# A two-layer streaming step with four mixers: first loads of POOL behind the first weights, x turned in one go, and 64 stationary columns for the sampled tokens' values

## Chip, cores and metric

One NeuronCore of one Trainium2 chip. The metric is the device time of one execution in microseconds (us), all inputs read from HBM and all outputs written to HBM. Everything is fp32.

## What is computed

The reference runs two layers over 256 prompt tokens and 64 sampled tokens (width 1024), the sampled ones with a cache of 512 latents and with recurrent states. Cut to one layer:

```
h = rms(x, norm_mix);  proj = h @ w_in            # 1024 -> 2984, split into 14 parts
y_a = rglru(causal_conv(lru_x))                   # gated linear recurrence
q = rms(q_lat) @ wq_b;  kv = [past_ckv, rms(kv_lat)] @ wkv_b
y_b = softmax(q k^T) v                            # latent attention, 4 heads
y_c = retention(rope(r_q), rope(r_k), r_v)        # 4 heads, state 64x64
y_d = mlstm(m_q, m_k, m_v, gates)                 # 4 heads, state 64x64
x = x + [head_rms(y_a..y_d) * gates] @ w_out
x = x + (silu(g) * u) @ w_down,  [g, u] = rms(x, norm_ffn) @ w_gu
```

The outputs are x for both token groups and each layer's new latents and states.

## The kernel before

The 320 tokens are kept feature by token: `xT` and `hT` hold 8 tiles of 128 features by 320 tokens. The tokens count as three tiles of 128, the last of which holds the 64 sampled ones and 64 unused places. Weights come in chunks of 256 columns (1 MB, two transfers on SP's queue) into `ring`, which has 5 slots; a slot is loaded again when TensorE has used it. Each engine has its program written out by hand, and semaphores with names order them: `step` makes an engine wait for its own last instruction, `need`, `claim`, `wait_filled` and `wait_chunk` wait for other engines, for a PSUM bank to be read, or for a chunk.

The start of the program is what most of the change touches:

- SP issues the transfers of x (second token tile and sampled tile, in two halves of 512 features: `x_loaded0`, `x_loaded1`), the chunk `ql` (weights of the query latents, the first weights used), seven small row loads, then the chunks `kvr`, `mo`, `mv`, `mq`. ACT issues the first token tile of x and the identity matrix. POOL issues the latents' loads (`load_latents`: `pckv`, `wqb`, `wkvb`), four blocks of the mLSTM state (`cin`), the first part of the constants (680 KB), four small gains, twelve small tables and the rest of the constants (1664 KB). Queue q0 is POOL's, q1 SP's, q10 ACT's.
- PE turns x into PSUM by matmuls with the identity (`turn_x`, L706), DVE copies each turned tile to `xT` (L1552), ACT squares it into `hT` (L1275), and PE sums the squares with a matrix of ones (`first_sum`, L712) into `ms1`. ACT makes `rstd` of that, DVE writes the normalised `hT` tile by tile (L1556), and PE starts on `ql0` and `ql1` (`feature`, L740).
- Then PE turns the rows of small vectors (L835) and the cached latents (`past_latents`, L805), multiplies these with `wkvb` (`latents_out`, L820), turns `cin` (L845), and goes on with `kvr` (L853), `mo`, the gate rows (L863), `mv`, ..., `mq`. Before `mq` it waits for all of the tables.

Later, in each layer, `weigh_values` (from L1017) multiplies the turned softmax weights `pT` with the values `vb` of one head; tile 2, the sampled tokens, takes five matmuls (L1021, L1023), and `b_out` on DVE scales the result into `ybm`. An fp32 matmul shows as two MATMUL records in the trace, and as one row with its repetitions in the lists of order below.

Of the kernel before, what the change touches and what calls it, by code (L numbers as in the profile page):

```python
# [16 lines left out]
ALU = mybir.AluOpType  # L17
# [4 lines left out]
P = 128  # L22
# [180 lines left out]
def build(nc, I, O):  # L203
    with ExitStack() as ctx:
# [15 lines left out]
        def C(name, rows=P):  # L220
            a, n = cat[name]
            return cst[0:rows, a:a + n]
# [119 lines left out]
        rows = gate[0:NROWS, 0, 0:P]  # L342
        cin = dhf[:, 0:DEPTH * 256].rearrange("p (l k a d) -> p l k a d", l=DEPTH, k=2, a=2)
        yst = sb("yst", [P, 6, NT * H])
# [242 lines left out]
        def _(pool):  # L587
# [40 lines left out]
            for l in range(DEPTH):  # L628

                if l == 0:  # L630
                    load_latents(0)
                    pool.wait_ge(sem("cleared_small"), 5)
                    for cdst, csrc in CIN:
                        pool.dma_start(cdst, csrc, allow_slow_non_contiguous=True).then_inc(sem("cin_loaded"), 16)
                    c1 = cat["negmask"][0]
                    pool.dma_start(cst[:, 2 * P:c1], I["consts"][:, 2 * P:c1]).then_inc(sem("consts_loaded"), 16)
                    for cdst, csrc in SMALL[0:4]:
                        pool.dma_start(cdst, csrc, allow_slow_non_contiguous=True).then_inc(sem("gains_loaded"), 16)
# [51 lines left out]
        def _(pe):  # L690
# [7 lines left out]
            for _ in range(WARM):  # L698
                mm(ps[:, 7, 0:P], dmx[:, 0:P], dmx[:, 0:P], start=True, stop=True)
            pe.wait_ge(sem("ident_loaded"), 16)  # L700
            pe.wait_ge(sem("x_cleared"), 1)
            def turn_x(ks):
                pe.wait_ge(sem(f"x_loaded{ks[0] // (KT // 2)}"), 48)
# [5 lines left out]
            def first_sum(ks):  # L709
                for k in ks:  # L710
                    need(pe, "squared", 0, 2 * KT, k + 1)
                    ins = mm(bank("ms1", 0, T), C("ones"), hT[:, k, 0:T], start=(k == 0), stop=(k == KT - 1),  # L712
                             skip_group_check=True)
                return ins
# [16 lines left out]

            def feature(use, l, name, c, m, cn=256, wait_h=False):

                claim(pe, use, l)
                wait_chunk(pe, name, l)
                w = chunk(name, l, cn)
                for k in range(KT):
# [3 lines left out]
                fill(ins, use)  # L741

# [65 lines left out]
            for l in range(DEPTH):  # L808
# [20 lines left out]

                for p in range(2):  # L830
                    feature(f"ql{p}", l, "ql", p * P, P, wait_h=(p == 0))
                if l == 0:
                    pe.wait_ge(sem("rows_loaded"), 16 * len(ROWLOADS))
                    pe.wait_ge(sem("x_turned"), KT)
                    nc.tensor.transpose(ps[:, 7, 0:NROWS], rows[:, :], ident[0:NROWS, 0:NROWS]).then_inc(  # L835
                        sem("rows_turned"), 1)
                    past_latents(0)
# [3 lines left out]
                    pe.wait_ge(sem("cin_loaded"), 16 * len(CIN))  # L841
                    wait_bank_read(pe, "ms1", l)
                    for ll in range(DEPTH):
                        for p in range(2):
                            ins = nc.tensor.transpose(ps[:, 3, (2 * ll + p) * P:(2 * ll + p + 1) * P],  # L845
                                                      cin[:, ll, p].rearrange("q a d -> q (a d)"), ident)
                    ins.then_inc(sem("rows_turned"), 1)
                claim(pe, "kvr", l)
# [7 lines left out]
                for p in range(2):  # L856
                    feature(f"mo{p}", l, "mo", p * P, P)
                for u, a in (("mig", 0), ("mfg", H)):
# [27 lines left out]
                if l == 0:  # L886
                    pe.wait_ge(sem("small_loaded"), 16 * len(SMALL[4::2]))
                    pe.wait_ge(sem("tables_loaded"), 16 * (len(SMALL[5::2]) + 1))
                    pe.wait_ge(sem("consts_loaded"), 16)
                for p in range(2):  # L890
# [122 lines left out]
                def weigh_values(h):  # L1013
# [228 lines left out]
        def _(act):  # L1242
            step = stepper(act, "act_chain")
            A = nc.scalar.activation
            act.dma_start(xtm[:, 0, 0:D // 2], I["x_prompt"][0, 0:P, 0:D // 2]).then_inc(sem("x_loaded0"), 16)
            act.dma_start(cst[:, 0:2 * P], I["consts"][:, 0:2 * P]).then_inc(sem("ident_loaded"), 16)
            act.dma_start(xtm[:, 0, D // 2:D], I["x_prompt"][0, 0:P, D // 2:D]).then_inc(sem("x_loaded1"), 16)
# [40 lines left out]
            for l in range(DEPTH):  # L1288
# [24 lines left out]
                if l > 0:  # L1313
                    key_stats(PAST_TILES[2:], 2)
                latent_squares(1)
                if l == 0:
                    past_copy(0)
                    key_stats(PAST_TILES, 0)
# [11 lines left out]
                if l == 0:  # L1330
                    act.wait_ge(sem("lam_abs"), 1)
                    A(lamt[:, 1, :], lamt[:, 0, :], ACT.Exp, scale=-1.0).then_inc(sem("lam_exp"), 1)
# [144 lines left out]
                if l == 0:  # L1477
                    act.wait_ge(sem("c8"), 1)
                for t in range(2):
# [58 lines left out]
        def _(dve):  # L1538
# [62 lines left out]
            def lam_tables():  # L1601

                lam = cols[:, ROWS["lam"]:ROWS["lam"] + DEPTH * 2]
                step(v.scalar_tensor_tensor(out=lamt[:, 0, :], in0=lam, scalar=-1.0, in1=lam, op0=ALU.mult, op1=ALU.max), "lam_abs")
                step(v.memset(gq[:, :], SCALE))
# [15 lines left out]
                step(v.tensor_scalar(c8[:, :], acc, -LRU_C, None, ALU.mult))  # L1621
                step(v.tensor_scalar(c16[:, :], acc, -2 * LRU_C, None, ALU.mult), "c8")

# [6 lines left out]
            for l in range(DEPTH):  # L1630
# [54 lines left out]
                for p in range(2):  # L1685
# [14 lines left out]
                                     bcn[:, l, KVR:KVR + ROPE].unsqueeze(1).broadcast_to([P, NT, ROPE]), ALU.mult))  # L1700
                if l == 0:
                    dve.wait_ge(sem("consts_loaded"), 16)
                c2, sn, lo, hi = rope_t(None, None, False)
# [176 lines left out]
                def b_out(h):  # L1880
# [274 lines left out]
```

## Time and profile before

| | |
|---|---|
| median of 3 runs | 963.48 us (963.4 to 963.54) |
| the profiled execution's own time | 963.5 us |
| its span | 961.7 us |
| PE busy | 944.8 us, 98% |
| DVE / ACT / POOL busy | 503.9 / 203.5 / 392.8 us |
| DMA | 112.12 MB, mean 117 GB/s |

The span is what the profiler sees between the first and the last instruction; the device time is 1.8 us longer. An engine's busy time leaves out register, wait and DMA-issuing instructions. "PEclk" is the clock that TensorE was granted, as a share of 2.4 GHz.

### The profile page before, as it was taken

What the parts mean: (1) busy time and instruction counts of PE and PEld (TensorE: products, weight loads), DVE (VectorE), ACT (ScalarE), POOL (GpSimd) and SP (SyncE); (2) the same over time, 40 slices, a digit from 0 to 9 for tenths busy, and PEclk for the clock granted to TensorE, in tenths of its full rate; (3) what the DMA queues carried; (4) which work ended last, traced back from release to release, by engine and by line L of the source; (5) the groups of instructions that cost most, each with busy time, mean ns of one, the idle gap of its engine ahead of it and who ended that gap; (6) DMA issues with size and microseconds to landing.
All of it is one profiled execution on the core that took longest, in us unless ns stands there. A gap on an engine that the chain in (4) does not pass through costs nothing. (4 is left out here: it accounts for less than half of the span.)

```text
span 961.7 us, 14966 instructions
## 1 busy us (share of the span) xinstructions
PE 944.8 (98%) x5786; PEld 827.6 (86%) x5786; DVE 503.9 (52%) x1028; ACT 203.5 (21%) x444; POOL 392.8 (41%) x383
## 2 busy tenths in 40 slices
PE   6999999999999999999999999999999999999998
PEld 4766777777999999999977677777789999999997
DVE  5355566772666565722253546568456565654321
ACT  2123244523110000100030243444321100001001
POOL 7010020032686666666511003001249666666770
PEclk8999999999999999999999999999999999999999
DMA  9832221125854444434424221121185544444421
GB/s 244 269 122 88 68 70 45 46 49 126 206 146 132 132 132 144 141 133 132 138 88 140 88 88 50 45 89 50 14 219 148 145 133 132 132 133 140 135 98 34
DMA packets 159042, 112.12 MB, mean 117 GB/s; under 512 B 10102, under 2 KB 156956, under 8 KB 158844
## 3 DMA queue, kind: packets, MB, share of 16 engines
q1 hardware_dynamic: 154388, 104.50, 37.7%
q0 software_dynamic: 3952, 5.92, 2.3%
q8 instruction: 46, 0.75, 0.3%
q10 hardware_dynamic: 632, 0.75, 0.3%
q14 instruction: 24, 0.20, 0.1%
HBM read 108.89 MB, written 2.27 MB: 116 GB/s over the span
## 5 line engine op out<-in xcount | busy, mean ns | idle before, releaser
L740 PE MATMUL ps<-hT,ring 128*128 128x320 f32 x672 | 189.5, 438 | 7.0 <-DMA ring<-in_w_in 6.7
L740 PEld LDWEIGHTS ps<-hT,ring 128*128 128x128 f32 x672 | 126.5, 192 | 61.0 <-issue 10.0
L604 POOL TENSOR_TENSOR work<-ring 128x512 f32<-128x512 f32 (+1 forms) x66 | 81.8, 1239 | 154.9 <-issue 112.4
L1105 PE MATMUL ps<-mixT,ring 128*128 128x160 f32 x672 | 105.0, 299 | 0.0
L1105 PE MATMUL ps<-hT,work 128*128 128x160 f32 x672 | 98.5, 299 | 0.0
L1105 PE MATMUL ps<-hT,ring 128*128 128x160 f32 x672 | 98.1, 299 | 0.0
L1105 PEld LDWEIGHTS ps<-mixT,ring 128*128 128x128 f32 x672 | 95.8, 190 | 0.0
L1105 PEld LDWEIGHTS ps<-hT,ring 128*128 128x128 f32 x672 | 93.7, 190 | 0.3
L1105 PEld LDWEIGHTS ps<-hT,work 128*128 128x128 f32 x672 | 93.7, 190 | 0.0
L605 POOL TENSOR_TENSOR ring<-ring 128x512 f32<-128x512 f32 (+1 forms) x66 | 82.5, 1250 | 5.2
L606 POOL TENSOR_TENSOR work<-ring 128x512 f32<-128x512 f32 (+1 forms) x66 | 81.9, 1241 | 5.2
L607 POOL TENSOR_TENSOR work<-ring,work 128x512 f32<-128x512 f32 (+1 forms) x66 | 81.8, 1239 | 5.2
L1510 ACT ACTIVATE arena<-ps 128x160 f32<-128x160 f32 x42 | 12.7, 303 | 286.9 <-PE ps L1105 286.9
L1062 PE MATMUL ps<-mixT,ring 128*128 128x320 f32 x256 | 71.1, 434 | 0.0
L2096 DVE TENSOR_TENSOR arena<-arena,ps 128x160 f32<-128x160 f32 x8 | 2.6, 321 | 121.6 <-ACT arena L1528 121.6
L1062 PEld LDWEIGHTS ps<-mixT,ring 128*128 128x128 f32 x256 | 48.0, 190 | 19.3
L615 POOL DMA_DIRECT2D out_p_ret<-sst x8 | 4.2, 528 | 143.7 <-DVE sst L1954 143.7
L1105 PE MATMUL ps<-work,ring 128*128 128x160 f32 x352 | 55.6, 299 | 0.0
L1105 PE MATMUL ps<-mixT,work 128*128 128x160 f32 x336 | 52.5, 299 | 0.0
L1105 PE MATMUL ps<-arena,ring 128*128 128x160 f32 x352 | 51.7, 299 | 0.0
L1105 PE MATMUL ps<-arena,work 128*128 128x160 f32 x352 | 51.7, 299 | 0.0
L1105 PEld LDWEIGHTS ps<-work,ring 128*128 128x128 f32 x352 | 50.4, 190 | 0.0
(387 smaller groups left out, 1388.5 us busy)
## 6 DMA issues: line engine op xcount, KB each, us to landing
ring<-in_w_gu SPq DMA_DIRECT2D x88, 512.0 KB, 5.2
ring<-in_w_in SPq DMA_DIRECT2D x44, 512.0 KB, 4.7
ring<-in_w_down SPq DMA_DIRECT2D x32, 512.0 KB, 4.4
ring<-in_w_out SPq DMA_DIRECT2D x16, 512.0 KB, 4.4
ring<-in_w_down SPq DMA_DIRECT2D x16, 384.0 KB, 3.7
cst<-in_consts POOLq DMA_DIRECT2D x1, 1664.0 KB, 13.4
ring<-in_w_in SPq DMA_DIRECT2D x2, 640.0 KB, 12.6
wqb<-in_mla_wq_b POOLq DMA_DIRECT2D x2, 384.0 KB, 7.8
```

The source lines that it names most:

```text
L604: step(tt(s3, a11, a21, ALU.subtract))
L605: step(tt(a21, a21, a22, ALU.add))
L606: step(tt(s2, a21, a11, ALU.subtract))
L607: step(tt(s4, a12, s2, ALU.subtract), "mixed")
L615: pool.dma_start(dst, src, allow_slow_non_contiguous=True).then_inc(sem("out_done"), 16)
L740: ins = mm(bank(use, 0, T, m), w[:, k, c:c + m], hT[:, k, 0:T], start=(k == 0), stop=(k == KT - 1))
L1062: ins = mm(bank(u, 0, T), w[:, k, (n % 2) * P:(n % 2 + 1) * P], mixT[:, k, :], start=(k == 6), stop=(k == 5), skip_group_check=True)
L1105: ins = mm(bank(use, at * HT, HT), left, right(k), start=(opens and k == 0 and at == 0), stop=(closes and k == n - 1), skip_group_check=True)
L1510: step(A(p1c[:, j % 2, :], bank(f"fa{j}", 0, HT), ACT.Copy), "p1_copied")
L2096: step(v.tensor_tensor(u2, p1, bank(ya, HT, HT), ALU.add))
```

## The change

POOL adds two pairs of squared tiles (0 with 1, 2 with 3), then waits for the chunk `ql`, and only then issues its loads. PE turns both halves of x before it sums, and sums six tiles in place of eight, two of them the added pairs. `ql1` is split after its sixth feature tile, and the cached latents are turned in between; `cin` lies in `ytm` in place of `dhf` and is turned behind `mo`. The four gains count on the same semaphore as the first constants, and DVE waits for both where it waited for the gains. The gate rows of tile 2 are turned with all 128 rows. In `weigh_values` tile 2 has 64 stationary columns in place of 128, and `b_out` writes it with an instruction of its own. DVE clears the unused half of that tile of `ybm` once, at the start. Some semaphores are merged.

```diff
-        cin = dhf[:, 0:DEPTH * 256].rearrange(...)
+        cin = ytm[:, :, :, :].rearrange("p t h e -> p (t h e)")[:, 0:DEPTH * 256].rearrange(...)
...
                 if l == 0:
+                    for n in range(2):
+                        pool.wait_ge(sem("squared"), 2 * n + 2)
+                        step(nc.gpsimd.tensor_tensor(hT[:, 2 * n, 0:T], hT[:, 2 * n, 0:T], hT[:, 2 * n + 1, 0:T], ALU.add),
+                             "sq_pairs")
+                    wait_chunk(pool, "ql", 0)
                     load_latents(0)
...
-            turn_x(range(0, KT // 2))
-            claim(pe, "ms1", 0)
-            first_sum(range(0, 3))
-            turn_x(range(KT // 2, KT))
-            fill(first_sum(range(3, KT)), "ms1")
+            turn_x(range(0, KT // 2))
+            turn_x(range(KT // 2, KT))
+            claim(pe, "ms1", 0)
+            for n, k in enumerate((0, 2, 4, 5, 6, 7)):
+                if n < 2:
+                    pe.wait_ge(sem("sq_pairs"), n + 1)
+                else:
                     need(pe, "squared", 0, 2 * KT, k + 1)
+                ins = mm(bank("ms1", 0, T), C("ones"), hT[:, k, 0:T], start=(k == 0), stop=(k == KT - 1))
+            fill(ins, "ms1")
...
-                for p in range(2):
-                    feature(f"ql{p}", l, "ql", p * P, P, wait_h=(p == 0))
+                feature("ql0", l, "ql", 0, P, wait_h=True)
+                feature("ql1", l, "ql", P, P, ks=range(0, 6))
+                if l == 0:
+                    past_latents(0)
+                feature("ql1", l, "ql", P, P, ks=range(6, KT))
...
-                        w_ = P if t < 2 else DEC
-                        ins = nc.tensor.transpose(bank(u, t * P, w_, H), mift[0:w_, t, a:a + H], ident[0:w_, 0:w_])
+                        ins = nc.tensor.transpose(bank(u, t * P, P, H), mift[:, t, a:a + H], ident)
...
                     for i in range(4):
-                        mm(bank(u, 128, 64), pT[:, 512 + i * P:512 + (i + 1) * P], vb[:, 3 + i, h, :],
+                        mm(bank(u, 128, 64, DEC), pT[:, 512 + i * P:512 + i * P + DEC], vb[:, 3 + i, h, :],
                            start=(i == 0), stop=False)
-                    fill(mm(bank(u, 128, 64), pT[0:64, 384:512], vb[0:64, 2, h, :], start=False, stop=True), u)
+                    fill(mm(bank(u, 128, 64, DEC), pT[0:64, 384:384 + DEC], vb[0:64, 2, h, :], start=False, stop=True), u)
...
+            step(v.memset(ybm[DEC:P, 2, :, :], 0.0))
...
                 if l == 0:
-                    dve.wait_ge(sem("gains_loaded"), 16 * 4)
+                    dve.wait_ge(sem("consts_loaded"), 16 * 5)
...
-                    step(v.tensor_tensor(ybm[:, :, h, :], bank(f"bo{h}", 0, 192).rearrange("p (t e) -> p t e", t=NT),
-                                         rs3.unsqueeze(2).broadcast_to([P, NT, HD]), ALU.mult), bank_read=(f"bo{h}", l))
+                    step(v.tensor_tensor(ybm[:, 0:2, h, :], bank(f"bo{h}", 0, 128).rearrange("p (t e) -> p t e", t=2),
+                                         rs3[:, 0:2].unsqueeze(2).broadcast_to([P, 2, HD]), ALU.mult))
+                    step(v.tensor_scalar(ybm[0:DEC, 2, h, :], bank(f"bo{h}", 128, 64, DEC), rs3[0:DEC, 2:3], None, ALU.mult),
+                         bank_read=(f"bo{h}", l))
```

PE's instructions at the start of the program, before: L706 turns x, L712 sums the squares, L813 and L835 turn rows of gains, L740 is `ql`, then `mo`, L805 turns the latents, L820 multiplies them, L845 turns `cin`, L853 is `kvr`.

```order
L706 MATMUL ps<-cst,arena 128x128 x12
L712 MATMUL ps<-hT,cst 128x320 x3
L706 MATMUL ps<-cst,arena 128x128 x12
L712 MATMUL ps<-hT,cst 128x320 x5
L813 MATMUL ps<-cst,work 128x16
L740 MATMUL ps<-hT,ring 128x320 x16
L835 MATMUL ps<-cst,work 128x108
L805 MATMUL ps<-cst,pckv 128x128 x4
L820 MATMUL ps<-wkvb,work 128x512 x4
L845 MATMUL ps<-cst,work 128x128 x4
L853 MATMUL ps<-ring,hT 128x168 x24
L740 MATMUL ps<-hT,ring 128x320 x16
```

The same place in the changed program, where the line numbers are a little higher (L710 turns x, L721 sums, L743 is `feature`, L809 turns the latents, L862 turns `cin`):

```order
L710 MATMUL ps<-cst,arena 128x128 x24
L721 MATMUL ps<-hT,cst 128x320 x6
L817 MATMUL ps<-cst,work 128x16
L743 MATMUL ps<-hT,ring 128x320 x14
L809 MATMUL ps<-cst,pckv 128x128 x4
L743 MATMUL ps<-hT,ring 128x320 x2
L842 MATMUL ps<-cst,work 128x108
L824 MATMUL ps<-wkvb,work 128x512 x4
L852 MATMUL ps<-ring,hT 128x168 x24
L743 MATMUL ps<-hT,ring 128x320 x16
L862 MATMUL ps<-cst,work 128x128 x4
```

The second turning stands ahead of all sums, the latents are turned two matmuls before `ql1` ends, and `cin` is turned behind `mo`.

POOL's instructions after its clearing, before (L622 to L626 are the latents, L634 `cin`, L636 the first constants, L638 the gains):

```order
L610 MEMSET wx 128x512
L622 DMA pckv<-in_cache_mla_ckv 128x4x128
L624 DMA wqb<-in_mla_wq_b 128x2x384
L626 DMA wkvb<-in_mla_wkv_b 128x512
L634 DMA work<-in_state_mlstm_C 64x2x64 x4
L636 DMA cst<-in_consts 128x1360
L638 DMA bcn<-in_mla_kv_norm 128x2x128
```

And in the changed program, where L633 is the adding of the pairs:

```order
L610 MEMSET wx 128x512
L633 ISA
L633 TENSOR_TENSOR hT<-hT 128x320 x2
L622 DMA pckv<-in_cache_mla_ckv 128x4x128
L624 DMA wqb<-in_mla_wq_b 128x2x384
L626 DMA wkvb<-in_mla_wkv_b 128x512
L639 DMA work<-in_state_mlstm_C 64x2x64 x4
L641 DMA cst<-in_consts 128x1360
L643 DMA bcn<-in_mla_kv_norm 128x2x128
```

The loads keep their order; two additions and the wait for `ql` stand ahead of all of them.

## Rows read from the trace of the kernel before

**Rows 1.** The page's busy times.

```profile
PE 944.8 (98%) x5786; PEld 827.6 (86%) x5786; DVE 503.9 (52%) x1028; ACT 203.5 (21%) x444; POOL 392.8 (41%) x383
```

**Rows 2.** PE's timeline: start, length, group, repetitions, idle before and its releaser.

```profile
6.49 1.50 PE L706 MATMUL ps<-cst,arena 128*128 128x128 f32 x12 [0.38 <-DMA arena<-in_x_sample]
...
10.96 1.47 PE L706 MATMUL ps<-cst,arena 128*128 128x128 f32 x12
...
21.99 10.83 PE L740 MATMUL ps<-hT,ring 128*128 128x320 f32 x32 [6.69 <-DMA ring<-in_w_in]
...
34.15 3.67 PE L820 MATMUL ps<-wkvb,work 128*128 128x512 f32 x8 [0.79 <-issue]
...
38.09 7.01 PE L853 MATMUL ps<-ring,hT 128*128 128x168 f32 x48
...
54.35 0.53 PE L863 MATMUL ps<-cst,mift 128*4 128x128 f32 x3 [0.28 <-DVEq L435]
...
69.18 17.39 PE L740 MATMUL ps<-hT,ring 128*128 128x320 f32 x64
```

**Rows 3.** Windows of 5 us: length, busy time of each engine, PEclk, DMA share, GB/s.

```profile
20.00:25.00 5.00, 3.01 (x6) 2.04 (x7) 0.92 (x2) 0.00 (x0) 0.00 (x0) 0.50 1.17 236
```

**Rows 4.** DMA queues, stretches 6:8, 10:12, 18:20: packets, MB, share of 16 engines.

```profile
q1 hardware_dynamic: 370, 0.51, 100.9%
...
q0 software_dynamic: 176, 0.54, 74.5%
q1 hardware_dynamic: 177, 0.17, 27.2%
...
q0 software_dynamic: 118, 0.13, 30.1%
```

**Rows 5.** DMA issues at 2.4, 3.5 and 4.4 us: KB each, us to landing.

```profile
arena<-in_x_sample SPq DMA_DIRECT2D x1, 128.0 KB, 6.5
...
ring<-in_w_in SPq DMA_DIRECT2D x1, 512.0 KB, 18.2
...
wkvb<-in_mla_wkv_b POOLq DMA_DIRECT2D x1, 256.0 KB, 8.5
```

**Rows 6.** Timelines of DVE and ACT at the start.

```profile
7.13 2.06 DVE L1552 COPY xT<-ps 128x320 f32<-128x320 f32 x4 [0.76 <-PE ps L706]
...
16.29 4.66 DVE L1556 SCALAR_TENSOR_TENSOR hT<-xT,cols,rstd 128x320 f32<-128x320 f32 x8 [0.69 <-ACT rstd L1259]
...
7.71 2.04 ACT L1275 ACTIVATE hT<-xT 128x320 f32<-128x320 f32 x4 [0.83 <-DVE xT L1552]
```

**Rows 7.** POOL's timeline: the issues of its loads.

```profile
2.76 0.92 POOL L622 DMA_DIRECT2D pckv<-in_cache_mla_ckv  x1
...
4.38 0.58 POOL L626 DMA_DIRECT2D wkvb<-in_mla_wkv_b  x1
...
17.70 0.65 POOL L641 DMA_DIRECT2D cst<-in_consts  x1
```

**Rows 8.** POOL's groups by form: busy us, mean ns of one, idle before.

```profile
L604 POOL TENSOR_TENSOR work<-ring 128x384 f32<-128x384 f32 x8 | 8.0, 1000 | 6.9 <-issue 4.6 <-POOL work L607 2.3
```

**Rows 9.** PE's timeline around `weigh_values` and two other groups; "128*64" is rows*columns stationary.

```profile
119.26 0.52 PE L787 MATMUL ps<-work 128*65 128x64 f32 x6
119.61 0.93 PE L930 MATMUL ps<-cst,arena 128*96 128x128 f32 x7
...
151.95 1.06 PE L1021 MATMUL ps<-arena 128*128 128x64 f32 x8
152.94 0.43 PE L1023 MATMUL ps<-arena 64*128 64x64 f32 x2
153.30 0.97 PE L930 MATMUL ps<-cst,arena 128*96 128x128 f32 x7
...
186.86 0.56 PE L787 MATMUL ps<-work 128*64 128x64 f32 x6
187.35 0.88 PE L796 MATMUL ps<-cst,work 128*128 128x128 f32 x6
```

More of the change, by code:

```diff
@@ L342, in build @@
         rows = gate[0:NROWS, 0, 0:P]
-        cin = dhf[:, 0:DEPTH * 256].rearrange("p (l k a d) -> p l k a d", l=DEPTH, k=2, a=2)
+        cin = ytm[:, :, :, :].rearrange("p t h e -> p (t h e)")[:, 0:DEPTH * 256].rearrange("p (l k a d) -> p l k a d", l=DEPTH, k=2, a=2)
         yst = sb("yst", [P, 6, NT * H])
@@ L637, in _ @@
                     for cdst, csrc in SMALL[0:4]:
-                        pool.dma_start(cdst, csrc, allow_slow_non_contiguous=True).then_inc(sem("gains_loaded"), 16)
+                        pool.dma_start(cdst, csrc, allow_slow_non_contiguous=True).then_inc(sem("consts_loaded"), 16)
                     for cdst, csrc in SMALL[5::2]:
@@ L699, in _ @@
                 mm(ps[:, 7, 0:P], dmx[:, 0:P], dmx[:, 0:P], start=True, stop=True)
-            pe.wait_ge(sem("ident_loaded"), 16)
             pe.wait_ge(sem("x_cleared"), 1)
             def turn_x(ks):
-                pe.wait_ge(sem(f"x_loaded{ks[0] // (KT // 2)}"), 48)
+                pe.wait_ge(sem(f"x_loaded{ks[0] // (KT // 2)}"), 64 if ks[0] == 0 else 48)
                 for k in ks:
@@ L707, in turn_x @@
                     ins.then_inc(sem("pre_filled"), 1)
-            def first_sum(ks):
-                for k in ks:
-                    need(pe, "squared", 0, 2 * KT, k + 1)
-                    ins = mm(bank("ms1", 0, T), C("ones"), hT[:, k, 0:T], start=(k == 0), stop=(k == KT - 1),
-                             skip_group_check=True)
-                return ins
-            turn_x(range(0, KT // 2))
-            claim(pe, "ms1", 0)
-            first_sum(range(0, 3))
-            turn_x(range(KT // 2, KT))
-            fill(first_sum(range(3, KT)), "ms1")
+            turn_x(range(0, KT // 2))
[5 more added lines that the diff above has]
+                else:
+                    need(pe, "squared", 0, 2 * KT, k + 1)
+                ins = mm(bank("ms1", 0, T), C("ones"), hT[:, k, 0:T], start=(k == 0), stop=(k == KT - 1))
+            fill(ins, "ms1")
             def norm_sum(use, l):
@@ L730, in norm_sum, with feature @@
                 fill(ins, use)
[L732 to L737, printed above, removed]
+            def feature(use, l, name, c, m, wait_h=False, ks=range(KT)):
+                if ks[0] == 0:
+                    claim(pe, use, l)
+                    wait_chunk(pe, name, l)
+                w = chunk(name, l, 256)
+                for k in ks:
                     if wait_h:
@@ L740, in feature @@
                     ins = mm(bank(use, 0, T, m), w[:, k, c:c + m], hT[:, k, 0:T], start=(k == 0), stop=(k == KT - 1))
-                fill(ins, use)
+                if ks[-1] == KT - 1:
+                    fill(ins, use)
             def value_tiles(which, l, p):
@@ L836, in _ @@
                         sem("rows_turned"), 1)
-                    past_latents(0)
                     pe.wait_ge(sem("cols_ready"), 2)
@@ L840, in _ @@
                     latents_out(PAST_TILES)
[L841 to L847, printed above, removed]
                 claim(pe, "kvr", l)
@@ L857, in _ @@
                     feature(f"mo{p}", l, "mo", p * P, P)
+                if l == 0:
+                    pe.wait_ge(sem("cin_loaded"), 16 * len(CIN))
+                    wait_bank_read(pe, "ms1", l)
+                    for ll in range(DEPTH):
+                        for p in range(2):
+                            ins = nc.tensor.transpose(ps[:, 3, (2 * ll + p) * P:(2 * ll + p + 1) * P],
+                                                      cin[:, ll, p].rearrange("q a d -> q (a d)"), ident)
+                    ins.then_inc(sem("rows_turned"), 1)
                 for u, a in (("mig", 0), ("mfg", H)):
@@ L888, in _ @@
                     pe.wait_ge(sem("tables_loaded"), 16 * (len(SMALL[5::2]) + 1))
-                    pe.wait_ge(sem("consts_loaded"), 16)
+                    pe.wait_ge(sem("consts_loaded"), 16 * 5)
                 for p in range(2):
@@ L1245, in _ @@
             act.dma_start(xtm[:, 0, 0:D // 2], I["x_prompt"][0, 0:P, 0:D // 2]).then_inc(sem("x_loaded0"), 16)
-            act.dma_start(cst[:, 0:2 * P], I["consts"][:, 0:2 * P]).then_inc(sem("ident_loaded"), 16)
+            act.dma_start(cst[:, 0:2 * P], I["consts"][:, 0:2 * P]).then_inc(sem("x_loaded0"), 16)
             act.dma_start(xtm[:, 0, D // 2:D], I["x_prompt"][0, 0:P, D // 2:D]).then_inc(sem("x_loaded1"), 16)
@@ L1314, in _ @@
                     key_stats(PAST_TILES[2:], 2)
+                if l == 0:
+                    past_copy(0)
                 latent_squares(1)
                 if l == 0:
-                    past_copy(0)
                     key_stats(PAST_TILES, 0)
@@ L1330, in _ @@
                 if l == 0:
-                    act.wait_ge(sem("lam_abs"), 1)
+                    act.wait_ge(sem("lam"), 1)
                     A(lamt[:, 1, :], lamt[:, 0, :], ACT.Exp, scale=-1.0).then_inc(sem("lam_exp"), 1)
@@ L1477, in _ @@
                 if l == 0:
-                    act.wait_ge(sem("c8"), 1)
+                    act.wait_ge(sem("lam"), 2)
                 for t in range(2):
@@ L1603, in lam_tables @@
                 lam = cols[:, ROWS["lam"]:ROWS["lam"] + DEPTH * 2]
-                step(v.scalar_tensor_tensor(out=lamt[:, 0, :], in0=lam, scalar=-1.0, in1=lam, op0=ALU.mult, op1=ALU.max), "lam_abs")
+                step(v.scalar_tensor_tensor(out=lamt[:, 0, :], in0=lam, scalar=-1.0, in1=lam, op0=ALU.mult, op1=ALU.max), "lam")
                 step(v.memset(gq[:, :], SCALE))
@@ L1621, in lam_tables @@
                 step(v.tensor_scalar(c8[:, :], acc, -LRU_C, None, ALU.mult))
-                step(v.tensor_scalar(c16[:, :], acc, -2 * LRU_C, None, ALU.mult), "c8")
+                step(v.tensor_scalar(c16[:, :], acc, -2 * LRU_C, None, ALU.mult), "lam")
             def state_tables():
```

2 lines of the change are left out of this document (removed).

## Prediction, made before the changed kernel ran

> **What bounds the kernel now.** I read the busy times of the page first: PE works 944.8 us of a span of 961.7 us [rows 1], so only some 17 us of the span are PE standing idle, and everything else is worth what it takes off PE or lets PE start sooner. The timeline of PE shows where those 17 us are: one gap of 6.69 us ahead of `ql0`, put down to the DMA of the first weights, is the only large one; the others in these rows are under 0.8 us [rows 2]. Behind that gap PE is slow for a while: `ql0` and `ql1`, 32 records, take 10.83 us, where 64 like them take 17.39 us later, 0.272 us each, which would be 8.7 us for 32 [rows 2]. The window from 20 to 25 us shows why: a granted clock of 0.50, the lower level of 1.2 GHz, after PE had done nothing since about 15.3 us [rows 3]. So late weights cost the wait and 2.1 us more.
>
> The DMA views say why the weights are late. The second half of `ql` was issued at 3.5 us and took 18.2 us to land, at 21.7 us [rows 5]. From 6 to 8 us SP's queue is alone but for crumbs and moves 370 packets, 0.51 MB, at a full share of the engines; from 10 to 12 us POOL's and SP's queues move 176 and 177 packets, packet for packet, and SP's gets 0.17 MB of it [rows 4]. POOL's packets are large (0.54 MB in 176), so POOL's loads hold `ql` back.
>
> **When `ql` lands with POOL's loads behind it.** The sampled half of x, issued last before `ql`, landed at 2.4 + 6.5 = 8.9 us [rows 5]. I take 8 us as the point where `ql` has the engines to itself, with some 0.88 of its 1.05 MB left. At 0.51 MB in 2 us that takes 3.5 us; with 0.8 us of my own on top for its landing to be signalled, 12.3 us. At the shared rate of 0.17 MB in 2 us [rows 4] it would be 18 us, which is the other bound. I take 12.3, since nothing of POOL's is under way.
>
> **When PE can use it.** Before, the second turning of x began at 10.96 us [rows 2], behind three sums; its data was there at 8.9. Now it begins at 8.9, 2.06 us earlier, and behind it stand 6 sums in place of 5, 2 records of 0.27 us more. Normalising therefore moves by 2.06 - 0.54 - 0.1 = 1.4 us, from 16.29 [rows 6] to 14.9. The pairs are ready: ACT's first four squares run from 7.71 to 9.75 us [rows 6], and an addition of POOL costs 1.0 us at 384 columns [rows 8], so at most that at 320; the second is done by 10.8, when PE, which turns x until 10.2, wants it at 10.75. The new clearing on DVE has the 0.76 us idle ahead of the first copy as cover [rows 6]; without it the copies would move by its length, 0.3 us at most. `ql0` starts one normalised tile behind 14.9, at 15.6 us, and `ql` has been there for 3 us. PE stands still for under 2 us ahead of it (before, 6.69), so I expect the clock to stay at 1.0.
>
> **From there to `kvr`.** `ql0` is now paced by DVE: 8 tiles in 4.66 us [rows 6], so it ends near 20.1. Six tiles of `ql1`, 12 records, end at 23.4. The latents must be in: POOL's issues move from 2.76 to 12.3, by 9.5 us, and `wkvb` (issued at 4.38, 8.5 us to land, so in at 12.9 [rows 5, 7]) lands at 22.4. It is 1 us ahead of PE. Then 0.44 us of turning (12 such records took 1.5 us less an overlap, 0.11 each [rows 2]), 4 records of `ql1` 1.1 us, and the turning and copying of the columns, for which I keep the 0.79 us that PE waited before `latents_out` [rows 2]: it starts at 25.7. Before, 34.15 to 38.09 was 3.94 us with 0.43 us for `cin` in it; without that `kvr` starts at 29.2, where it started at 38.09 [rows 2]. That is **8.9 us**. `cin`'s 0.43 us comes back behind `mo`, where part of it fills the wait of 0.28 us on DVE at 54.35 [rows 2]; I charge 0.2. **Start: -8.7 us.** Turning the gate rows with 128 rows changes two records by less than 0.1 us, nothing.
>
> What else is queued behind POOL's wait: `cin` (PE now wants it at 45), the first constants and gains (DVE's normalised latents, which run behind `kvr`, past 36) and the tables (PE ahead of `mq`, 69.18 [rows 2], now 60.5). POOL's last issue was at 17.70 [rows 7]; 9.5 us later it is 27.2. All have 10 us or more of cover even if they took twice as long to land as `wkvb`. If one were late, its wait would stand on PE in full.
>
> **The sampled values.** From the first record of L1021 to the instruction behind L1023 it is 153.30 - 151.95 = 1.35 us, of which L1023 takes 0.36 [rows 9]. Groups with 64 or 65 stationary columns show what narrower ones cost. Six records with 65 take 119.61 - 119.26 = 0.35 us, 0.058 each; six with 64, between groups of another width, take 187.35 - 186.86 = 0.49 us, so changing width costs something: 0.14 inside and behind the group, and I take 0.10 ahead of it [rows 9]. Eight records now: 0.10 + 0.49 + 2 x 0.058 = 0.71. L1023's two fall by the same 0.06 each, to 0.24. Together 0.95 in place of 1.35: 0.40 us a head, 8 heads, **-3.2 us**. Bounds: 0.49 / 6 for every record gives 0.10 + 0.65 + 0.36 = 1.11, so -1.9 us; no cost of changing gives 0.46 + 0.24 = 0.70, so -5.2. The Trainium skill (TensorE: Matmul & The Clock Gate, LDWEIGHTS) has a weight load scale with the columns, P / 1.2 ns: an estimate by it is 53 ns less for each of 10 loads, 0.53 us a head, and -4.3 us in all; it knows of no price for the change of width, which the six records with 64 columns show. PE has no wait of size in these stretches, so I let all of it count. DVE's second instruction in `b_out` adds some 0.2 us a head beside PE; DVE is busy half of the time [rows 1], and nothing on PE waits for `b_out` but two turnings that stand far behind.
>
> **Sum.** -8.7 - 3.2 = -11.9 us against the profiled execution's 963.5, which is the median of the runs too (963.48): **951.6 us**.
>
> **Rivals.**
> *The latents come late.* They are wanted at 23.4 us, and 1 us of cover is little. For it: SP's queue has `kvr`, `mo` and more standing ready now, and from 18 to 20 us POOL's queue moved only 0.13 MB in 2 us [rows 4]; at that pace the 0.9 MB of latents take 14 us and land at 17 + 14 = 31, PE waits 7.5 us, and its clock may fall (2 us): 959 to 961. Against it: at that time POOL's queue had mostly tiny tables, and with bulk it moved 0.54 MB in 2 us beside SP's. Chance 0.11, with a milder form (1 to 4 us late) in it, 953 to 956.
> *`ql` lands no earlier*, since its own queue and not POOL's share holds it: the 0.17 MB in 2 us. Then POOL's loads start near 20 us, the latents land near 30, and PE, ready for them at 28, waits 2 us: the start gains nothing, and the time is 963.5 - 3.2 = 960 to 961. The 0.51 MB of 6 to 8 us speaks against it. Chance 0.04.
> *The clock falls* in the gap ahead of `ql0`: 2.1 us as before, 953.7. The gap is a third of the old one. Chance 0.07.
> *Slower.* The same lateness of the latents decides here: PE turns them in order, with `ql1`'s end, `kvr` and all behind. The kernel gets slower when they land later than 23.4 + 11.9 = 35.3 us, 13 us behind my estimate; each us beyond is one on the time. With bulk sent from 17 us on even the slowest stretch shown ends by 31. Chance 0.03, about 966.
>
> **How the numbers follow.** Forecast 0.75 (its own range 949.5 to 953.5: the bounds of the values, and 1 us of x's or POOL's additions). The range 948.8 to 956.5 takes in the clock and the mild form of late latents, and leaves out the rest. What a measurement can tell from no change is 0.2%, 1.9 us: all cases but the last are faster by more, save a bit of the first two. Faster 0.94, same 0.03, slower 0.03.
>
> **What would show it.** In the changed profile: the second half of `ql` lands by 13 us; PE's first `feature` record starts near 15.6 with a clock of 1.0 through 30 us; L809 has no idle time on DMA ahead of it; `kvr` starts near 29.2; no wait before `mq`; from the first 64-column record to the instruction behind it 0.95 us. It would be wrong if the two queues' share is not what delays `ql`, if POOL's loads take over 10 us to land, if POOL's first additions are slow to begin, or if changing the width costs more than 0.14 us each way.

## The result, and the profile after

The changed kernel takes **951.63 us** (median of 4 runs, 951.55 to 952.01), against 963.44 us (962.84 to 963.54) for the kernel before on the same chip: a ratio of 0.9879, 95% interval 0.9862 to 0.9897. The profiled execution took 951.66 us, 1.8 us more than its span. The forecast was 951.6. One execution of experiment 5 (2533.38 us) and one of experiment 8 (3206.92 us) stand far off all the others; they hardly move the medians, and the ratios leave them out.

Busy times from the page of the changed kernel (PE is TensorE's matmuls, PEld its weight loads):

```profile
span 949.9 us, 14970 instructions
PE 938.3 (99%) x5782; PEld 821.2 (86%) x5782; DVE 505.4 (53%) x1037; ACT 203.6 (21%) x444; POOL 394.4 (42%) x385
```

The span is 11.8 us shorter than before, PE's busy time 6.5 us shorter [rows 1]. The other 5.3 us are idle time of PE that is no longer there. PE's timeline at the start shows it (start, length, what it did, and in brackets the idle time ahead of it with what ended that); L710 turns x, L721 sums, L743 is `feature`, L809 turns the latents, L824 multiplies them, L852 is `kvr`, L862 turns `cin`:

```profile
6.29 1.50 PE L710 MATMUL ps<-cst,arena 128*128 128x128 f32 x12 [0.67 <-DMA cst<-in_consts]
8.55 1.53 PE L710 MATMUL ps<-cst,arena 128*128 128x128 f32 x12 [0.76 <-DMA arena<-in_x_sample]
9.92 3.65 PE L721 MATMUL ps<-hT,cst 128*128 128x320 f32 x12
...
15.43 8.06 PE L743 MATMUL ps<-hT,ring 128*128 128x320 f32 x28 [1.70 <-DVE hT L1564]
23.32 0.60 PE L809 MATMUL ps<-cst,pckv 128*128 128x128 f32 x4
23.76 1.24 PE L743 MATMUL ps<-hT,ring 128*128 128x320 f32 x4
...
25.51 3.70 PE L824 MATMUL ps<-wkvb,work 128*128 128x512 f32 x8 [0.41 <-DVE cols L1668]
29.05 7.00 PE L852 MATMUL ps<-ring,hT 128*128 128x168 f32 x48
...
44.50 0.60 PE L862 MATMUL ps<-cst,work 128*128 128x128 f32 x4
...
46.06 8.88 PE L743 MATMUL ps<-hT,ring 128*128 128x320 f32 x32 [0.26 <-DVE work L1699]
...
60.25 17.39 PE L743 MATMUL ps<-hT,ring 128*128 128x320 f32 x64
```

The gap of 6.69 us for the first weights [rows 2] is one of 1.70 us, and it ends with a tile from DVE, no longer with a DMA. `ql0` starts 6.56 us earlier, `kvr` 9.04 us earlier, `mv` 8.92 and `mq` 8.93 us earlier than in [rows 2]. What lies between 6.56 and 9.04 is the clock, for the most part, then `cin`, which is now turned later, and the idle time ahead of `latents_out`, 0.41 us in place of 0.79 [rows 2]. From 20 to 25 us the granted clock had been 0.50 [rows 3]. The row of that window is now (length, busy time of PE, PEld, DVE, ACT, POOL, then PEclk, DMA share and GB/s):

```profile
20.00:25.00 5.00, 5.00 (x22) 3.40 (x21) 0.00 (x0) 1.03 (x2) 5.00 (x9) 1.00 1.25 292
```

The DMA queues (packets, MB, share of 16 engines), first from 10 to 12 us and then from 16 to 18 us. The share is the sum of what the packets took, each counted in full in the window in which it starts, so it can pass 100%:

```profile
q1 hardware_dynamic: 962, 0.64, 114.1%
...
q0 software_dynamic: 112, 0.41, 63.8%
q1 hardware_dynamic: 278, 0.27, 46.5%
```

Where SP's queue had 0.17 MB of 0.71 MB beside POOL's [rows 4], it now moves 0.64 MB alone. The DMA issues at the start (KB of each, us from issue to landing), the second half of `ql` and `wkvb`:

```profile
ring<-in_w_in SPq DMA_DIRECT2D x1, 512.0 KB, 7.9
...
wkvb<-in_mla_wkv_b POOLq DMA_DIRECT2D x1, 256.0 KB, 7.1
```

`ql`'s half took 18.2 us before and `wkvb` 8.5 us [rows 5]. POOL's own timeline, its second addition and the first and third of the latents' issues:

```profile
9.70 0.86 POOL L633 TENSOR_TENSOR hT<-hT 128x320 f32<-128x320 f32 x1 [0.25 <-ACT hT L1281]
12.10 0.93 POOL L622 DMA_DIRECT2D pckv<-in_cache_mla_ckv  x1 [1.54 <-DMA ring<-in_w_in]
...
13.74 0.58 POOL L626 DMA_DIRECT2D wkvb<-in_mla_wkv_b  x1
```

So `wkvb` is in at 13.74 + 7.1 = 20.8 us, 2.5 us before PE wants it at 23.32. And PE around one head of `weigh_values`; L1027 and L1029 are the sampled tokens' matmuls:

```profile
142.29 0.39 PE L1024 MATMUL ps<-arena 128*128 128x64 f32 x2
142.51 0.39 PE L1025 MATMUL ps<-arena 128*128 128x64 f32 x2
142.83 0.68 PE L1027 MATMUL ps<-arena 128*64 128x64 f32 x8
143.44 0.33 PE L1029 MATMUL ps<-arena 64*64 64x64 f32 x2
143.69 0.97 PE L936 MATMUL ps<-cst,arena 128*96 128x128 f32 x7
```

From L1027 to the instruction behind L1029 it is 0.86 us, and L1025 takes 0.32 us until L1027 starts, 0.10 more than the 0.22 before it (142.29 to 142.51): 0.96 us where it had been 1.35.

### The profile page after: what moved, and what is told of

It is laid out like the page before. It is cut to its first block and busy times, and to the rows that moved or that the text cites. A ratio compares the mean times of both kernels' runs of the same rounds, so it can differ in the third digit from the quotient of the medians.

```text
span 949.9 us, 14970 instructions
## 1 busy us (share of the span) xinstructions
PE 938.3 (99%) x5782; PEld 821.2 (86%) x5782; DVE 505.4 (53%) x1037; ACT 203.6 (21%) x444; POOL 394.4 (42%) x385
## 5 line engine op out<-in xcount | busy, mean ns | idle before, releaser
L743 PE MATMUL ps<-hT,ring 128*128 128x320 f32 x672 | 187.9, 435 | 2.2 <-DVE hT L1564 1.7
L743 PEld LDWEIGHTS ps<-hT,ring 128*128 128x128 f32 x672 | 124.9, 190 | 56.2 <-DVE hT L1564 3.9
```

## The experiments

Every run is set against the kernel before on its own chip, which took 963.1 to 963.6 us there.

**1. Before, with only POOL's wait for `ql` added.**

```diff
                 if l == 0:
+                    wait_chunk(pool, "ql", 0)
                     load_latents(0)
```

> The kernel before, with one line added: POOL waits for the chunk ql before its first load; nothing else of the change. If POOL's loads are what holds ql back, ql lands near 12 us, ql0 starts one tile behind the normalising at 17.0 us (it starts at 16.3, since x is turned as before), the clock stays at 1.0, and PE reaches the latents' products near 27.3 in place of 34.15: 6.9 us gained, 956.6 us. If ql's own queue sets its landing, PE starts ql0 near 22 us still and the kernel stays at 963 to 964 us or gets slower by the late latents. If waiting alone does it and the early turning of x adds nothing, the time is below 955.5.

Measured: 957.22 us against 963.18 (its four executions lie from 956.86 to 960.17), ratio 0.9944 (0.9927 to 0.9962), 0.6 us over the expectation. Its PE timeline:

```profile
17.03 9.13 PE L741 MATMUL ps<-hT,ring 128*128 128x320 f32 x32 [1.70 <-DVE hT L1557]
...
31.44 7.01 PE L854 MATMUL ps<-ring,hT 128*128 128x168 f32 x48
```

`ql`'s second half lands 7.8 us after its issue, and `kvr` starts 6.65 us earlier than in [rows 2]. This one line is half of the whole gain: 6.0 of 11.8 us by the medians, 6.6 by the spans of the profiled executions (955.1 against 961.7). The two queues' share is what delayed `ql`.

**2. Before, with both halves of x turned ahead of all sums.**

```diff
             turn_x(range(0, KT // 2))
-            first_sum(range(0, 3))
             turn_x(range(KT // 2, KT))
-            fill(first_sum(range(3, KT)), "ms1")
+            fill(first_sum(range(0, KT)), "ms1")
```

> The kernel before, with both halves of x turned ahead of all eight sums; POOL's loads stay where they were, no pairs are added. Theory: rstd is ready some us earlier, but ql lands at 21.7 us as before, so ql0 starts at 22 us and the time is 963.4 us, within 0.3. Rival: the start of PE's work is set by x as much as by ql, so that 1 us or more is gained, 962.4 or less.

Measured: 963.32 us against 963.18, ratio 1.0 (0.999 to 1.0009). PE:

```profile
10.24 4.47 PE L712 MATMUL ps<-hT,cst 128*128 128x320 f32 x16
...
21.62 11.90 PE L739 MATMUL ps<-hT,ring 128*128 128x320 f32 x32 [6.75 <-DMA ring<-in_w_in]
```

The sums end sooner and the weights come when they come. In this execution `ql` even started 0.37 us earlier, and its 32 records took 11.90 us in place of 10.83: the clock was down before the weights were there (0.76 from 15 to 20 us, 0.92 before). Work that ends sooner ahead of a fixed wait gives nothing by the medians, and in this one execution the slow stretch behind it was longer.

**3. The change without POOL's additions, 8 sums in place of 6.**

```diff
-                    for n in range(2):
-                        pool.wait_ge(sem("squared"), 2 * n + 2)
-                        step(nc.gpsimd.tensor_tensor(hT[:, 2 * n, 0:T], hT[:, 2 * n, 0:T], hT[:, 2 * n + 1, 0:T], ALU.add),
-                             "sq_pairs")
...
-            for n, k in enumerate((0, 2, 4, 5, 6, 7)):
-                if n < 2:
-                    pe.wait_ge(sem("sq_pairs"), n + 1)
-                else:
-                    need(pe, "squared", 0, 2 * KT, k + 1)
+            for k in range(KT):
+                need(pe, "squared", 0, 2 * KT, k + 1)
```

> The changed kernel without POOL's two additions: PE sums all eight squared tiles, behind both turnings; POOL still waits for ql. Theory: PE's sums are a packed row of records that sets rstd, so two sums more cost four records of 0.27 us: ql0 starts 1.1 us later and the time is 952.7 us. Rival: the squares of ACT set the end of the sums, so the pairs are worth nothing and the time stays at 951.6 us.

Measured: 952.54 us against 963.18, ratio 0.9889 (0.9874 to 0.9903), 0.9 us over the change. The sums take 4.47 us in place of 3.65, and `ql0` starts at 16.32 in place of 15.43. The additions are worth what PE saves, and once the weights are early all of it counts.

**4. The change with 128 stationary columns again.**

```diff
-                        mm(bank(u, 128, 64, DEC), pT[:, 512 + i * P:512 + i * P + DEC], vb[:, 3 + i, h, :],
+                        mm(bank(u, 128, 64), pT[:, 512 + i * P:512 + (i + 1) * P], vb[:, 3 + i, h, :],
...
-                    fill(mm(bank(u, 128, 64, DEC), pT[0:64, 384:384 + DEC], vb[0:64, 2, h, :], start=False, stop=True), u)
+                    fill(mm(bank(u, 128, 64), pT[0:64, 384:512], vb[0:64, 2, h, :], start=False, stop=True), u)
```

> The changed kernel with weigh_values and b_out as before: 128 stationary columns for the sampled tokens. Theory: each head loses 0.40 us again, and gets back the 0.1 us that PE waits longer for DVE in one place of each layer: 954.6 us. By the rule of weight loads alone (53 ns a load) it would be 955.9; if the narrower columns did nothing beyond the noise, 951.6.

Measured: 954.6 us against 963.18, ratio 0.991 (0.9893 to 0.9926): the start alone is worth 8.6 us, and the columns 3.0.

**5. The change with the fifth matmul over all 128 rows** (DVE clears the rows of `pT` that it now reads, once a layer).

```diff
-                    fill(mm(bank(u, 128, 64, DEC), pT[0:64, 384:384 + DEC], vb[0:64, 2, h, :], start=False, stop=True), u)
+                    fill(mm(bank(u, 128, 64, DEC), pT[:, 384:384 + DEC], vb[:, 2, h, :], start=False, stop=True), u)
...
+                step(v.memset(pT[HD:P, 384:384 + DEC], 0.0))
```

> The changed kernel, in which the fifth matmul of the sampled tile also takes all 128 rows (the lower 64 rows of its weights cleared by one DVE instruction a layer), so that five alike stand in a row, 128 rows by 64 columns. If it is the change of shape that costs, and not the matmuls, the changes ahead of and behind the 64-row pair shrink to one: 0.15 us a head, 1.2 us less, 950.5 us. If the record's own width is all that counts, nothing changes: 951.6. If the clearing on DVE stands in the way, 952 or more.

Measured: 950.77 us against 963.09, ratio 0.9873 (0.9856 to 0.9889), the fastest version of all. PE in the same head:

```profile
142.82 0.68 PE L1027 MATMUL ps<-arena 128*64 128x64 f32 x8
143.34 0.28 PE L1029 MATMUL ps<-arena 128*64 128x64 f32 x2
143.55 0.97 PE L936 MATMUL ps<-cst,arena 128*96 128x128 f32 x7
```

0.73 us in place of 0.86, with twice the rows in the last matmul: whatever the fewer rows saved, the change from 128 to 64 rows cost more. That is 0.13 x 8 = 1.0 us; some 0.2 of it is given back, since PE waits for DVE a little longer at L978, the swap of halves between the heads (0.5 us in place of 0.4, once a layer).

**6. The change with the latents issued last of POOL's early loads**, behind `cin`, the first constants and the gains.

```diff
                     wait_chunk(pool, "ql", 0)
-                    load_latents(0)
...
                     for cdst, csrc in SMALL[0:4]:
                         pool.dma_start(cdst, csrc, allow_slow_non_contiguous=True).then_inc(sem("consts_loaded"), 16)
+                    load_latents(0)
```

> The changed kernel with the three loads of the latents issued behind cin, the first constants and the gains, 6.0 us later on POOL's queue. Theory of the prediction: wkvb then lands near 27.5 us, PE wants the latents at 23.3 and waits 4.2 us in the middle of ql1, all of which the end sees: 955.8 us, up to 957.5 if the clock falls in the wait. If the latents had cover enough, or the wait were made up behind it, 951.6.

Measured: 962.85 us against 963.09, ratio 0.9998 (0.9988 to 1.0007). The whole gain is gone, and the expectation missed by 7 us. PE:

```profile
31.85 1.09 PE L809 MATMUL ps<-cst,pckv 128*128 128x128 f32 x4 [8.35 <-DMA wkvb<-in_mla_wkv_b]
32.73 2.34 PE L743 MATMUL ps<-hT,ring 128*128 128x320 f32 x4
...
39.55 7.00 PE L852 MATMUL ps<-ring,hT 128*128 128x168 f32 x48
```

`wkvb`, issued at 19.65 us, took 12.1 us to land in place of 7.1. The wait is 8.35 us, the clock falls in it (0.62 from 25 to 30 us), and the four records behind take 2.34 us where they took 1.24. The window from 30 to 35 us:

```profile
30.00:35.00 5.00, 3.15 (x9) 2.15 (x9) 0.00 (x0) 0.60 (x1) 0.00 (x0) 0.50 1.16 244
```

`kvr` starts 10.5 us later than in the change: 8.35 of wait and 2.1 of clock. So the place of the latents in POOL's queue is what the gain hangs on. Why they took 12.1 us shows in the queues from 22 to 24 us:

```profile
q0 software_dynamic: 79, 0.09, 135.4%
q1 hardware_dynamic: 74, 0.07, 14.5%
```

79 packets of POOL's start there, take 135% of the 16 engines' 2 us and carry 0.09 MB: 1.354 x 32 / 79 = 0.55 us a packet, where the row of 16 to 18 us above has 0.638 x 32 / 112 = 0.18 us. Some of the loads ahead of the latents are slow for their size. Experiments 9, 10 and 12 look for which.

**7. The change without POOL's wait for `ql`**, so that its loads stand behind the squares alone.

```diff
-                    wait_chunk(pool, "ql", 0)
                     load_latents(0)
```

> The changed kernel without POOL's wait for the chunk ql; its loads still stand behind the two additions and so behind the fourth square, from 10.6 us in place of 12.1. Theory: POOL's queue moves its first bytes about 4 us after its first issue (12.1 to 15.9 us in the changed kernel), here at 14.4, while ql lands at 11.5, so the wait for ql decides nothing: 951.6 us. Rival: the wait is what protects ql; without it ql is late by 1 us or more and the time above 952.6, if it comes later than the 15.4 us at which PE wants it.

Measured: 951.68 us against 963.09, ratio 0.9883 (0.9869 to 0.9898), the same as the change. POOL's first issue stands at 11.26 us behind its second addition, its queue's first bytes move between 14 and 16 us, and `ql` is in by 12. It is the place behind the additions that protects `ql`; the wait itself decides nothing here.

**8. Before, with 28 matmuls of zeros ahead of `ql0`** to keep PE busy (they go to a bank that holds nothing then).

```diff
                         sem("rows_turned"), 1)
+                    pe.wait_ge(sem("x_turned"), KT)
+                    for _ in range(28):
+                        mm(ps[:, 7, 0:P], dmx[:, 0:P], dmx[:, 0:P], start=True, stop=True)
```

> The kernel before, with 28 matmuls of zeros on PE between the turning of the gains and ql0, some 6 us of work in a gap of 6.7 us; they compute nothing that is used. Theory: the granted clock stays at 1.0, ql0 and ql1 take 8.7 us in place of 10.8, and the time is 961.3 us: this is the clock's part of the late weights. Rival: the slow records come from the DMA load or from something else that is going on at 22 us, and the time stays at 963.3.

Measured: 961.26 us against 963.09, ratio 0.998 (0.997 to 0.9989). PE:

```profile
14.92 6.52 PE L817 MATMUL ps<-work 128*128 128x128 f32 x56
21.68 8.85 PE L740 MATMUL ps<-hT,ring 128*128 128x320 f32 x32 [0.24 <-DMA ring<-in_w_in]
```

```profile
20.00:25.00 5.00, 4.76 (x26) 3.65 (x26) 0.61 (x2) 0.00 (x0) 0.00 (x0) 1.00 1.13 245
```

The weights come hardly earlier, but the clock stays at 1.00 from 15 to 30 us and `ql` takes 8.85 us, not 10.83. The clock's part of the old gap is 1.8 to 2.0 us.

**9. The change with `cin` and the first constants (0.81 MB) ahead of the latents, the gains behind them.**

```diff
-                    load_latents(0)
                     pool.wait_ge(sem("cleared_small"), 5)
...
                     pool.dma_start(cst[:, 2 * P:c1], I["consts"][:, 2 * P:c1]).then_inc(sem("consts_loaded"), 16)
+                    load_latents(0)
```

> The changed kernel with cin and the first constants (0.81 MB) issued ahead of the latents, and the four gains behind them: the latents' issues move by 3.0 us. Theory: what made the latents so late in the run before was the gains, whose packets of 2048 bytes took over 1 us each; bulk ahead of the latents costs only its issues and its bytes. wkvb lands near 25 to 26.5 us, PE waits 2 to 3 us at the latents: 953.5 to 955 us. If it is bulk ahead of them, and not the gains, that makes the latents late, they land past 29 us: over 957.5.

Measured: 954.88 us against 963.12, ratio 0.9912 (0.9898 to 0.9927). PE:

```profile
25.88 0.63 PE L809 MATMUL ps<-cst,pckv 128*128 128x128 f32 x4 [2.00 <-DMA wkvb<-in_mla_wkv_b]
```

The only difference from experiment 6 is that the four gains' loads, 0.19 MB, no longer stand ahead: that takes the wait from 8.35 to 2.00 us. Of these 6.35 us the four issues' own time is 2.8 (`wkvb` is issued at 16.83 us and not at 19.65); 3.2 are a faster landing, 8.9 us after the issue in place of 12.1.

**10. The change with only the four gains' loads ahead of the latents.**

```diff
                     wait_chunk(pool, "ql", 0)
+                    for cdst, csrc in SMALL[0:4]:
+                        pool.dma_start(cdst, csrc, allow_slow_non_contiguous=True).then_inc(sem("consts_loaded"), 16)
                     load_latents(0)
```

> The changed kernel with the four gains (0.19 MB) issued ahead of the latents: the latents' issues move by 3.0 us, as with the constants, but with hardly a byte ahead of them. If only issues and bytes counted, wkvb would land at 20.9 + 3.0 = 23.9 us and PE wait 0.6 us: 952.2 us. If the gains' slow packets hold the engines that the latents need, it lands 2 to 4 us later than that, 26 to 28, and the time is 954.5 to 957, more than with the constants ahead although four times fewer bytes stand there.

Measured: 960.4 us against 963.12, ratio 0.9979 (0.9968 to 0.9989). The direction was as expected, the size above the range. PE, and the queues from 18 to 20 us:

```profile
29.62 1.09 PE L809 MATMUL ps<-cst,pckv 128*128 128x128 f32 x4 [6.26 <-DMA wkvb<-in_mla_wkv_b]
```

```profile
q0 software_dynamic: 21, 0.03, 97.4%
q1 hardware_dynamic: 121, 0.12, 19.7%
```

0.19 MB cost more than the 0.81 MB of experiment 9. The 21 packets that start there take 97% of all engines' 2 us, 1.5 us each. `wkvb`, issued at 16.53 us, landed 13.0 us later, where it took 8.9 in experiment 9.

**11. Before, with only the narrow columns** (L1017 on, `b_out` and its clearing, as in the change).

> The kernel before with the narrow columns alone: weigh_values and b_out of the changed kernel and the clearing of ybm; start and POOL as before. Theory: 8 heads at 0.40 us, less the 0.1 us that PE waits longer for DVE in each layer: 3.0 us less than before on the same chip, 960.2. If the two halves of the change help each other, it is less than 2 us.

Measured: 960.63 us against 963.12, ratio 0.9971 (0.9961 to 0.9981): 2.5 us, and 2.9 us by the spans of the profiled executions (958.8 against 961.7). With experiment 4 the columns are worth 2.5 to 3.0 us.

**12. The change with two of the four gains ahead of the latents.**

```diff
                     wait_chunk(pool, "ql", 0)
+                    for cdst, csrc in SMALL[1:3]:
+                        pool.dma_start(cdst, csrc, allow_slow_non_contiguous=True).then_inc(sem("consts_loaded"), 16)
                     load_latents(0)
...
-                    for cdst, csrc in SMALL[0:4]:
+                    for cdst, csrc in SMALL[0:1] + SMALL[3:4]:
```

> The changed kernel with two of the four gains' loads, in_mla_kr_norm and in_mla_qr_norm (32 KB each, one short row of HBM sent to all 128 partitions), ahead of the cached latents; the other two (in_mla_kv_norm 128 KB, and the small in_state_mlstm_m) stay where they were. With all four ahead, L809 waited 6.26 us for wkvb and the time was 960.4. Theory: it is the packets of these two short rows that hold the engines, so nearly all of that comes back: wkvb lands 11 to 12.5 us after its issue, L809 waits 4.5 to 6 us, clock below 1.0 behind the wait, 958 to 960. Rival 1: it is in_state_mlstm_m with its scattered elements (it landed last of the four in that run, 9.7 us). Then two issues of 0.75 us and 64 KB stay under the cover of 2.5 us: 951.6 to 952.2. Rival 2: it is the 128 KB of in_mla_kv_norm, the largest of the four: the same 951.6 to 952.2.

Measured: 958.47 us (5 runs, 957.75 to 960.75) against 963.58, ratio 0.9958 (0.9944 to 0.9972), 6.8 us over the change for 64 KB. PE, and the queues from 18 to 20 us:

```profile
27.94 0.63 PE L811 MATMUL ps<-cst,pckv 128*128 128x128 f32 x4 [4.46 <-DMA wkvb<-in_mla_wkv_b]
28.41 2.26 PE L745 MATMUL ps<-hT,ring 128*128 128x320 f32 x4
```

```profile
q0 software_dynamic: 14, 0.02, 102.2%
q1 hardware_dynamic: 160, 0.16, 24.7%
```

```profile
wkvb<-in_mla_wkv_b POOLq DMA_DIRECT2D x1, 256.0 KB, 12.5
```

`wkvb` took 12.5 us to land. The 14 packets took as much time as all engines have in 2 us, 1.022 x 32 / 14 = 2.3 us each. Asked for the two halves of that window, the trace puts 11 of the 14, with 204.2% of one us, between 18 and 19 us: 3.0 us each. From 19 to 20 us, while they are under way, SP's queue moves 45 packets and 0.05 MB. Over the 2 us it moves 0.16 MB, a quarter of the 0.64 MB that it moves alone. `in_state_mlstm_m` and `in_mla_kv_norm` stood behind the latents here, so neither is needed for the delay, and the two rivals fall. They add little even in experiment 10: `wkvb` lands 1.7 us later there (29.5 and 27.8 us), and 1.25 of that is its later issue (16.53 and 15.28). What is slow is the load of 32 numbers a layer, 128 bytes, spread from one place in HBM to 128 partitions. Whether it is the short runs or the one place that makes them slow was not tried.

In the changed kernel the same two loads stand behind the latents and land at 25.0 and 26.5 us. POOL's queue from 24 to 26 us reads:

```profile
q0 software_dynamic: 88, 0.09, 95.1%
```

So a stretch of costly packets is there too, but `wkvb` has landed by then and nothing on PE waits.

## Why the prediction was right, step by step

**`ql` with the engines to itself.** Forecast to land at 12.3 us, with 18 as the other bound. The second half, issued at 3.6 us (the prediction read 3.5), landed 7.9 us later, at 11.5, and POOL's first load was issued at 12.1. That is 8 + 3.5, without the 0.8 us that I had added for the signal and that no row had shown. Experiment 1 shows the mechanism alone. The rival that `ql` lands no earlier is dead.

**Turning x in one go, and the pairs.** The second turning began at 8.55 (forecast 8.9), normalising at 14.73 (14.9), `ql0` at 15.43 (15.6). POOL's additions took 0.87 us, under the bound of 1.0. The clearing on DVE hid in its idle time. The rows named in the prediction also leave out a wait of 1.25 us for ACT's squares ahead of the first sums before (L712, at 9.25 us), which went with the turning in one go. That the turning and the pairs work only together with the early weights the prediction implied by its chain. Experiment 2 shows the turning at 0 us alone; behind the early weights `ql0` starts at 15.43 us in place of experiment 1's 17.03, 1.6 us, of which experiment 3 gives 0.9 to the pairs. The rest of what experiment 4's start (8.6 us) has over experiment 1's (6.0) belongs to the split of `ql1`, which takes the wait ahead of `latents_out` from 0.80 to 0.41 us, and to the place of `cin`; no run tried these two by themselves.

**The clock.** Forecast at 1.0 behind a gap of under 2 us; it was 1.70 us and the clock stayed at 1.0. The 2.1 us that I read out of the records are 1.8 to 2.0 by experiment 8.

**The latents.** Here the place on the path was right and the cover was mis-sized: 1.0 us forecast, 2.5 us measured. The issue came 0.2 us sooner, and `wkvb` took 7.1 us, not the 8.5 of a time when x and `ql` were under way as well; that this is the reason was not tried. The rival that they come late did not happen, but its mechanism is real: experiments 6, 9, 10 and 12 give waits of 8.35, 2.00, 6.26 and 4.46 us and times of 962.9, 954.9, 960.4 and 958.5. What I had wrong in it is the point from which the kernel is slower. I put it at a landing of 35.3 us, with each us of lateness worth one; the clock's 2.1 us come on top, which puts it near 23.3 + 11.8 - 2.1 = 33.0. Experiment 6 fits that by the spans of the profiled executions, where a landing at 31.8 us leaves 1.4 us of the gain (960.3 against 961.7); by the medians (962.85 against 963.09) that landing already took all of it. And my bound for the slowest pace, 0.13 MB in 2 us on POOL's queue, is no bound: experiments 10 and 12 show 0.03 and 0.02 MB in 2 us.

**`kvr` and `cin`.** `kvr` at 29.05 us (forecast 29.2), `cin` 9.04 - 8.92 = 0.12 us (0.2). The start is 8.9 us of gain where 8.7 were forecast.

**The sampled values.** Forecast 0.95 us a head with 0.10 for entering the narrow group; measured 0.96, and the entry is 0.10. The estimate of 4.3 us by the rule of the Trainium skill (TensorE: Matmul & The Clock Gate, LDWEIGHTS) overstates what the kernel gains: experiments 4 and 11 measured 3.0 and 2.5. The eight heads gave 8 x 0.39 = 3.1 us, and 0.2 of that is missing at the end: PE's wait for DVE at L978 is 0.1 us longer in each layer (0.8 us in two waits, 0.6 before). "PE has no wait of size in these stretches, so I let all of it count" was right to 0.2 us.

**Sum.** 8.9 + 3.1 - 0.2 = 11.8 us, the difference of the spans; forecast 11.9. The two small misses, +0.2 at the start and -0.3 in the heads, cancel, so that the exact hit owes something to luck.

## What to carry to other kernels

When the first weights are late, look at which queue's bytes share the engines with them before looking at the weights' own issue; ordering another engine's loads behind an event that happens anyway can be worth more than any trimming of the work ahead, which gives nothing while the wait stands. A load that is pushed back must be followed to its first reader, with the clock's loss added to the wait, and small loads ahead of it are to be weighed by how long their packets hold the engines, not by their bytes. Grouping matmuls by the shape of their stationary operand can save more than trimming one of them: here a full-size fifth matmul was faster than a half-size one.

## What the runs showed of the hardware

- **Short rows sent to all partitions are expensive.** With 64 KB of them at the head of POOL's queue, its packets took 2.3 us each from 18 to 20 us (experiment 12), against 0.18 us when the latents and constants are under way, and they slow SP's queue as well: 0.16 MB in 2 us in place of 0.64.
- **The two queues often alternate packet for packet**: 176 to 177 [rows 4], 79 to 74 in experiment 6. The queue with large or slow packets then takes the larger share, 74.5% to 27.2% and 135.4% to 14.5%. The Trainium skill (DMA: Bandwidth & Descriptors, Queues, rings and completion order) has each DMA engine go round the queues that have work, a packet at a time, and these rows agree. The rows of experiments 10 and 12, 21 to 121 and 14 to 160 packets, do not show it; what POOL's queue had ready on each engine then is not in them.
- **POOL's queue is slow to begin.** In the changed kernel its first issue stands at 12.10 us; from 12 to 15.5 us its queue moves nothing and from 15.5 to 16 us two packets. The bulk comes from 16 us on (112 packets in the row of 16 to 18 us above). That is over 3 us to the first packets. The Trainium skill (DMA: Bandwidth & Descriptors, Specifications) gives about 1 us to the first byte on this path; the measurement decides, and it is longer here. SP's queue filled the engines meanwhile (119.2% from 12 to 14 us), and how much of the delay is a wait behind it no run separates. The late beginning also fits experiment 7, which loses nothing.
- **Changing the stationary operand's shape costs time of its own**: 0.10 us on going from 128 to 64 columns, and 0.13 us in all for having the last matmul over 64 rows and not 128 (experiment 5).
- **The clock and the length of an idle stretch of PE.** Behind 1.70 and 2.00 us of idle time the granted clock stayed at 1.0; behind 6.69 and 8.35 us it was at 0.50, the lower level of 1.2 GHz; behind 4.46 us it fell too: the four records behind the wait took 2.26 us, as in experiment 6 and not 1.24, and the means of the windows from 25 to 30 and from 30 to 35 us are 0.85 and 0.81. The loss was about 2 us behind the two long waits and some 1.5 us behind that of 4.46 (`kvr` 6.05 us later than in the change).
